# PSUM banks in the first block: two for the projections, six for the early heads, in place of three and five

## What is computed

```python
proj = u @ w_in[l]
qa, ka, va, qb, kb, vb, g = jnp.split(proj, SPLITS, axis=-1)
qa, ka, qb, kb = rope(qa), rope(ka), rope(qb), rope(kb)
o_swa = windowed_gqa_sink_attention(qa, ka, va, attn_sink[l], pos, is_real)
o_diff = differential_attention(qb, kb, vb, lam, lambda_init, diff_subln_gain[l], is_key)
gates = jax.nn.sigmoid(g + b_gate[l])
merged = g_swa * (o_swa @ w_branch_swa[l]) + g_diff * (o_diff @ w_branch_diff[l])
h = h + rms_norm(merged @ w_out[l], post_mix_gain[l])
```

## Time and profile before

| | us |
|---|---|
| median of the timed runs | 962.1 |
| span of the profiled execution, first to last instruction | 961.6 |
| mean granted TensorE clock | 0.996 of 2.4 GHz |
| PE busy | 939.9 (98%) |
| DVE busy | 675.0 (70%) |
| ACT busy | 527.5 (55%) |

### The profile page before, as it was taken

One profiled execution on the slowest core, in us unless ns is written; L12 is line 12 of the kernel. 1 busy time (PEld: TensorE's weight loads), 2 busy tenths in 40 slices (PEclk: granted clock), 3 DMA queues, 4 the chain that ended last, 5 costly groups with the idle time before them and its releaser, 6 DMA issues.

```text
span 961.6 us, 15483 instructions
## 1 busy us (share of the span) xinstructions
PE 939.9 (98%) x6180; PEld 841.4 (87%) x6180; DVE 675.0 (70%) x1233; ACT 527.5 (55%) x1013; POOL 137.8 (14%) x159
## 2 busy tenths in 40 slices
PE   8999999999999999999999999999999999999996
PEld 7999888999999988888888898897798898888885
DVE  6888777777578676766748669767665567676665
ACT  6876665775456644344446686555454454343443
POOL 2212111211133000000001129931000000000001
PEclk9999999999999999999999999999999999999998
DMA  9544324334377555454566563300543455656441
GB/s 315 185 150 133 132 88 145 119 132 133 132 245 238 166 207 202 172 197 174 186 205 203 169 233 131 127 6 1 176 147 119 150 175 176 219 175 216 168 142 45
DMA packets 115863, 154.71 MB, mean 161 GB/s; under 512 B 2728, under 2 KB 98224, under 8 KB 115536
## 3 DMA queue, kind: packets, MB, share of 16 engines
q1 hardware_dynamic: 113376, 142.91, 44.2%
q0 software_dynamic: 1952, 10.42, 2.9%
q10 hardware_dynamic: 464, 0.40, 0.1%
HBM read 150.56 MB, written 3.16 MB: 160 GB/s over the span
## 4 chain that ended last, share of the span: by engine, by line
PE 88%; DVE 4%; ACT 3%; POOL 3%; issue 1%; DMA 0%; POOLq 0%; DVEq 0%; ACTq 0%
PE ps L841 14%; PE ps L817 8%; PE ps L819 8%; PE ps L818 8%; PE ps L842 7%; PE ps L1129 4%; PE ps L860 4%; PE ps L862 4%; PE ps L861 4%; PE ps L1102 4%; PE ps L1103 4%; PE ps L1104 4%; PE ps L803 3%; PE ps L832 2%; PE ps L830 2%; PE ps L831 2%
## 5 line engine op out<-in xcount | busy, mean ns | idle before, releaser
L1368 DVE TENSOR_TENSOR wlo<-raw,whi 128x1024 fp32r<-128x1024 f32 (+1 forms) x268 | 327.9, 1242 | 166.3 <-ACT whi L1980 165.9
L1980 ACT ACTIVATE whi<-raw 128x1024 fp32r<-128x1024 f32 (+1 forms) x268 | 273.9, 1050 | 131.8 <-PE ps L842 53.5
L841 PE MATMUL ps<-R1b,whi 128*128 128x512 f32 x576 | 201.8, 393 | 0.0
L817 PE MATMUL ps<-R1b,whi 128*128 128x256 f32 (+1 forms) x592 | 172.3, 291 | 0.8 <-DVE wlo L1368 0.8
L819 PE MATMUL ps<-R1b,wlo 128*128 128x256 f32 (+1 forms) x592 | 167.7, 283 | 0.0
L818 PE MATMUL ps<-R1b,whi 128*128 128x256 f32 (+1 forms) x592 | 167.5, 283 | 0.0
L842 PE MATMUL ps<-R1b,wlo 128*128 128x256 f32 x576 | 161.4, 280 | 0.0
L841 PEld LDWEIGHTS ps<-R1b,whi 128*128 128x128 f32 x576 | 108.1, 188 | 24.7 <-issue 0.5
L817 PEld LDWEIGHTS ps<-R1b,whi 128*128 128x128 f32 x592 | 111.6, 188 | 9.1 <-issue 7.9
L819 PEld LDWEIGHTS ps<-R1b,wlo 128*128 128x128 f32 x592 | 111.8, 189 | 0.0
L818 PEld LDWEIGHTS ps<-R1b,whi 128*128 128x128 f32 x592 | 111.5, 188 | 0.2
(11 more groups left out here) (293 smaller groups left out, 1784.1 us busy)
## 6 DMA issues: line engine op xcount, KB each, us to landing
raw<-in_w_in SPq DMA_DIRECT2D x34, 1024.0 KB, 5.0
raw<-in_w_ffn_in SPq DMA_DIRECT2D x22, 1024.0 KB, 5.1
raw<-in_w_ffn_out SPq DMA_DIRECT2D x11, 1024.0 KB, 5.4
raw<-in_w_gate SPq DMA_DIRECT2D x11, 1024.0 KB, 5.1
raw<-in_w_up SPq DMA_DIRECT2D x11, 1024.0 KB, 5.2
raw<-in_w_down SPq DMA_DIRECT2D x11, 1024.0 KB, 5.5
raw<-in_w_out SPq DMA_DIRECT2D x8, 1024.0 KB, 5.1
raw<-in_w_xkv SPq DMA_DIRECT2D x8, 1024.0 KB, 5.4
```

What stands on the lines that cost most here:

```text
L817: e.matmul(o, hi[:, kt, c], R[0][:, kt, 0:n], start=kt == 0, stop=False)
L841: e.matmul(B[:, :].rearrange("p (a n) -> p a n", a=2), hi[:, kt, c], R[2][:, :, kt, 0:256], start=kt == 0, stop=False)
L1368: e.tensor_tensor(half_of(wlo[i % HL], i, k), half_of(raw[i % RAW], i, k), f32(half_of(whi[i % HL], i, k)), SUB).then_inc(lo_split(i, (i, k)))
L1980: return e.activation(o, i, f, **kw)
```

## The change

`gemm` shrinks to banks 0 and 1. A new pool `early` holds banks 2 to 7, and the tenants of the heads up to the fifth differential head (x below 13), the value transposes of va and those of vb with u below 3 use it. Later ones stay with `head`, banks 3 to 7. bdf 2 still takes bank 2.

```diff
-        pools = {"all": banks, "gemm": banks[0:3], "head": banks[3:8], "big": banks[0:2], "small": banks[2:8],
+        pools = {"all": banks, "gemm": banks[0:2], "head": banks[3:8], "early": banks[2:8], "big": banks[0:2], "small": banks[2:8],
...
             def vt(key, u, j):
-                B = claim("head", (key, u, j, "t"), (val_dve, (key, u, j)))
+                B = claim("early" if key == "va" or u < 3 else "head", (key, u, j, "t"), (val_dve, (key, u, j)))
...
+            def room_of(x):
+                return "early" if x < 13 else "head"
+
             def scores(x, t, Q, K, done):
...
-                    B = claim("head", ("score", x, u), done(u))
+                    B = claim(room_of(x), ("score", x, u), done(u))
...
-                    B = claim("head", ("PT", x, t), (head_dve if t else head_act, ("PT", x, t)))
+                    B = claim(room_of(x), ("PT", x, t), (head_dve if t else head_act, ("PT", x, t)))
...
-                    B = claim("head", ("O", x), (head_act, ("oh", x)), (head_dve, ("ol", x)))
+                    B = claim(room_of(x), ("O", x), (head_act, ("oh", x)), (head_dve, ("ol", x)))
...
-                    O = claim("head", ("O", x), (head_act, ("oh", x)), (head_dve, ("ol", x)))
-                    B = claim("head", ("PT", x), (head_act, ("PT", x)))
+                    O = claim(room_of(x), ("O", x), (head_act, ("oh", x)), (head_dve, ("ol", x)))
+                    B = claim(room_of(x), ("PT", x), (head_act, ("PT", x)))
```

## The result

The changed kernel takes 967.0 us (median of five runs, 966.0 to 967.4) against 962.1 (five runs, 961.95 to 963.6): 1.0047 times as long, 95% interval 1.0037 to 1.0058. I had forecast slower, by 2.6 us, with a range that ended at 965.8. It is slower by 4.9, so the sign and the place were right and the size was not.

The account below looks back on a forecast made before the run. TensorE was taken to bound the kernel, so only its idle time counts: + 2.67 us opening wait, - 1.3 heads, + 1.3 clock fall = + 2.6, giving a median of 964.7 us, range 963.0 to 965.8.

Parts of the forecast that it names:

- The place and the wait of the opening: Opening: rope 2 must wait for bank 0 until rope 0's cosine product ends, starting at 22.15, a loss of 2.67 us.
- The claims behind it: Opening, after rope 2: rope 3, value blocks and gate 0 find their banks free, gate 0 by 0.3 us; no loss.
- The fall of the clock: After the opening's 3.4 us idle piece, TensorE's clock likely falls to half for 3.4 us, costing 1.3 us.
- The heads' gain: Heads 5 to 8: the wait moves from third to fourth score, gaining 0.33 us each, 1.3 us in all.
- One score takes half of the 0.66 us: Head 6's scores behind the wait: each takes half of 0.66 us, so the fourth is due one score after the third.
- The span against the median: Whole run: the median of 962.1 is 0.5 us more than the profiled span of 961.6, and that part stays.
- four waits of 2.0 us: Third score matmuls of heads 5 to 8 waiting for ACT's copy: all that a larger heads' pool can win by.
- Rival A: Opening: the clock holds at full speed through the new wait; 963.4 us, chance 0.32.
- rival C: Opening: gate 0 and the value blocks also wait because ACT and DVE fall behind; 965.7 to 966 us, chance 0.08.

Follow-up runs that it names:

- e2_gemm2_alone: The kernel before with only the projections' pool cut to banks 0 and 1, heads left on banks 3 to 7: 967.14 us, ratio 1.0046.
- e3_fill_wait: The changed kernel with seven needless 256-wide matmuls (3.1 us) put ahead of rope 2's claim of bank 0: 964.24 us.
- e9_fill3: The changed kernel with three needless 256-wide matmuls in the opening's wait, leaving about 2.1 us idle: 965.8 us.
- after_again: The changed kernel run once more, unaltered, for the spread of its runs: 966.2 us.
- e6_after_fill_late: The changed kernel with needless 128-wide matmuls ahead of the two idle pieces at 673 and 676 us: 966.7 us.
- e5_pt1: The changed kernel with three banks for the opening's projections and, in heads 5 to 8, the fourth score on the bank DVE copies out: 959.84 us, ratio 0.9976.
- e10_swap5: The kernel before with, in heads 5 to 8, the third score on the bank DVE copies out and the fourth on ACT's: 962.41 us, ratio 1.0007.

## Why the prediction was right and wrong

- **The place and the wait of the opening: right.** Rope 2 at 22.15 forecast, 22.17 found, released by the cosine product of rope 0; 2.67 us forecast, 2.69 found. e2_gemm2_alone puts all of the loss there, and nothing absorbed it on the way to the end.
- **The claims behind it: nearly right.** Values and rope 3 start without idle time. Gate 0 was to be 0.3 us early and lost 0.23: the product that it needs started at 42.97 and ended at 43.39, with PE's last matmul ahead of it issued at 43.22. The fall of the clock isn't the reason, since it delays PE and the chain alike: in e3_fill_wait, without it, gate 0 loses the same 0.23. There the chain comes out as I had reckoned, free at 42.11 against 42.0. It is PE that is early, due at 41.94 + 0.12 = 42.06 (matmuls follow each other every 0.12 us there) and not 42.36, because head 0 had given back 0.39 us that my sum didn't have. The lines of e3_fill_wait, with PE's last matmul ahead of gate 0 and its first:

```profile
41.69 0.42 DVE L1456 TENSOR_TENSOR SD<-ps,ca 128x256 f32<-128x256 f32 x1
...
41.94 0.28 PE L819 MATMUL ps<-R1b,wlo 128*128 128x256 f32 x1
42.22 0.36 PE L817 MATMUL ps<-R1b,whi 128*128 128x256 f32 x1
```

- **The fall of the clock: right that it comes, its price mis-sized.** I took one stretch of 3.4 us, 1.3 us. By the profiles a short stretch costs 1.33 us where 0.4 us of it fall into the wait (after) and 1.5 where it begins behind the wait (e2_gemm2_alone, e9_fill3, after_again), and one twice as long costs 2.4 (e6_after_fill_late). By the medians the difference between e3_fill_wait and the change is 2.7 us in one set of runs and 2.0 in the other, which is 0.3 to 0.5 us more than the profiles give to the stretch; that rest isn't explained. By the times the clock is 0.7 to 1.4 us of the miss. I had no row for how the length of the stretch varies. The Trainium skill's "TensorE: Matmul & The Clock Gate", "Why this matters for your kernels", asks to avoid long idle gaps between matmul bursts. The runs agree: with the gap filled the kernel is 2.7 us faster.
- **The heads' gain: wrong, and this is the step that failed.** "One score takes half of the 0.66 us" put two scores one behind the other that run side by side: behind a release the next instruction comes after 0.66 us with two scores and 0.65 with one, and the fourth is due together with the third. Moving the wait from the third to the fourth score thus wins nothing: 1.3 us forecast, 0 found. e5_pt1 and e10_swap5 show that the end of the group moves with the last release. Small gains that I hadn't seen, 0.39 at head 0 and 0.30 at head 12, are of the same kind. The earlier trace rows has no line for these two, since PE was busy with the third score while the fourth was 0.29 and 0.2 us late; with 0.1 us of restart the groups took 1.51 us (35.24 to 36.75) and 1.42 (201.04 to 202.46) in place of 1.12. So four waits of 2.0 us weren't all that a larger pool could win by.
- **The span against the median: wrong.** I added 0.5 us for what lies around the span. It is 2.1, and the profiled execution of before was 1.6 us slower than its median, because of the low stretch at 677 us. I had that stretch in the earlier trace rows and used its price, but didn't ask whether the timed runs have it. The forecast of the median doesn't hang on this.

The sum by measurement: 962.0 + 2.7 (wait) + 0.2 (gate 0) - 0.4 (head 0) - 0.3 (head 12) = 964.2, which e3_fill_wait reads, and 1.8 to 2.7 for the clock by the times, 966.0 to 966.9. Against 964.7 the median of 967.0 is 2.3 more: 1.3 for heads 5 to 8, 1.4 for the clock and 0.2 for gate 0, less the 0.7 of heads 0 and 12. Those 0.7 us I had not forecast, so it is luck that the miss is no larger. Rival A, the clock holds, is out for this kernel (none of ten timed runs); rival C's mechanism, the claim of gate 0, is there but small.

## What to carry to other kernels

When a pool is made smaller, look first at the opening, where the readers of the banks are behind with other work, and compare for each claim the release with the start, as it worked here to 0.02 us. Price a wait by where the group behind it ends, from starts and not from the list of waits, and look first which matmuls of the group run side by side. A release that came 0.2 to 0.3 us late for one of a pair cost 0.3 to 0.4 us that no list shows, and moving a wait from one of the pair to the other wins nothing if the last release stays. And a wait of over 2 us on TensorE, where it bounds the kernel, may be paid twice, once as a wait and once in the clock behind it; matmuls that nobody needs put into it took the second part away.

## What the runs showed of the hardware

The granted clock doesn't fall for the same time in each execution: behind the same 3.5 us of idle time the low stretch lasted 3.4 us in one profiled execution (21.8 to 25.1) and 6.8 in another (20.95 to 27.76). With 2.17 us idle between dense runs it fell in the profiled execution of e9_fill3 and, by their times (964.4 and 964.5 us, mean clock 0.998), not in two others. The kernel before has two groups of timed runs that differ by 1.6 us, by the profiles because of one such stretch, so a difference of that size between a profile and a median is to be looked for in the clock before anything else.

Two score matmuls of 64 rows each, one on rows 0 to 63 and one on rows 64 to 127, with different banks to write, ran side by side: they start within 0.01 us of each other, and two of them take 0.66 us to the next instruction behind a wait where one takes 0.65. While one of the two ran, a wait of the other left no idle time in the trace (0.29 us at head 0 of before, 0.18 at head 6 of e5_pt1).

After a wait for a semaphore a score's second pass started 0.33 us behind its first, in place of the 0.23 of a second pair that doesn't wait. The 0.1 us is what such a wait cost beyond its own length. I didn't find out which part of PE's queue that time goes to.
